# Summing 40 of 72 modulation slots over their row tiles on VectorE in a two-layer diffusion trunk

## The reference, cut to what matters

```python
def adaln(cond, w, b):
    return (jax.nn.silu(cond) @ w + b)[:, None, :]
...
def pre_norm(x, mod, j, g):
    return rmsnorm(x, g) * (1 + mod_chunk(mod, 3 * j + 1)) + mod_chunk(mod, 3 * j)

def post_residual(x, out, mod, j, g, w):
    return x + w * mod_chunk(mod, 3 * j + 2) * rmsnorm(out, g)

def swiglu(h, w_in, w_out):
    gate, up = jnp.split(h @ w_in, 2, axis=-1)
    return (jax.nn.silu(gate) * up) @ w_out
```

## Time and profile before

| | before |
|---|---|
| median of 3 runs | 1670.7 us (1670.51 to 1671.05) |
| span of the profiled execution | 1671.3 us |
| TensorE busy | 1619.9 us, 97% |
| VectorE busy | 834.8 us, 50% |
| ScalarE busy | 695.4 us, 42% |
| DMA | 259.83 MB, mean 155 GB/s |

### The profile page before, as it was taken

How to read it: one execution, slowest core, us unless ns; L and a number is a source line. 1 busy time by engine, 2 the same in 40 slices (tenths; PEclk the granted TensorE clock), 3 DMA queues, 4 the chain that set the end, 5 groups by cost and what they waited for, 6 DMA issues and landing times.

```text
span 1671.3 us, 27671 instructions
## 1 busy us (share of the span) xinstructions
PE 1619.9 (97%) x11325; PEld 1577.4 (94%) x11325; DVE 834.8 (50%) x1323; ACT 695.4 (42%) x1205; POOL 41.9 (3%) x46
## 2 busy tenths in 40 slices
PE   5999999999998999999999999999999999999997
PEld 4999999999887988999999999999999999999997
DVE  5544434463456988443434744433462866343333
ACT  3433333353453456333333633334363356333332
POOL 2000000001100000000000000000000000000000
PEclk8999999999998999999999999999999999999998
DMA  9733366667983126433333633346453465333310
GB/s 326 232 126 125 126 214 221 209 202 220 282 277 101 51 89 192 140 128 127 116 128 126 202 126 125 125 135 193 136 193 126 146 203 181 126 125 119 114 45 38
DMA packets 255663, 259.83 MB, mean 155 GB/s; under 512 B 6625, under 2 KB 253826, under 8 KB 255570
## 3 DMA queue, kind: packets, MB, share of 16 engines
q1 hardware_dynamic: 249664, 251.67, 46.6%
q10 hardware_dynamic: 4978, 4.41, 0.8%
q0 software_dynamic: 928, 2.44, 0.6%
HBM read 255.88 MB, written 2.62 MB: 155 GB/s over the span
## 4 chain that ended last, share of the span: by engine, by line
PE 88%; DVE 7%; issue 2%; ACT 2%; POOL 1%; DMA 1%; ACTq 0%; DVEq 0%; POOLq 0%
PE bank L405 25%; PE bank L406 25%; PE bank L407 25%; PE bank L1454 3%; PE bank L1498 1%; PE bank L426 1%; PE bank L427 1%; PE bank L428 1%; DVE X L1054 1%; DVE WL L372 1%; PE bank L1724 1%; PE bank L1505 1%; DVE HL L1020 1%; ACT WH L358 1%; DVE SUMS L1310 1%
## 5 line engine op out<-in xcount | busy, mean ns | idle before, releaser
L372 DVE TENSOR_TENSOR WL<-RAW,WH 128x1024 fp32r<-128x1024 f32 (+1 forms) x335 | 401.2, 1199 | 693.4 <-ACT WH L358 692.9
L358 ACT ACTIVATE WH<-RAW 128x1024 fp32r<-128x1024 f32 (+1 forms) x344 | 358.2, 1045 | 651.3 <-PE bank L407 638.6
L405 PE MATMUL bank<-HH,WH 128*128 128x384 f32 x1664 | 562.3, 338 | 7.3 <-DVE WL L372 3.1
L406 PE MATMUL bank<-HL,WH 128*128 128x384 f32 x1664 | 559.9, 336 | 0.0
L407 PE MATMUL bank<-HH,WL 128*128 128x384 f32 x1664 | 559.8, 336 | 0.0
L405 PEld LDWEIGHTS bank<-HH,WH 128*128 128x128 f32 x1664 | 313.4, 188 | 10.3 <-DVE WL L372 3.7
L407 PEld LDWEIGHTS bank<-HH,WL 128*128 128x128 f32 x1664 | 313.4, 188 | 0.0
L406 PEld LDWEIGHTS bank<-HL,WH 128*128 128x128 f32 x1664 | 313.3, 188 | 0.0
L405 PE MATMUL bank<-AH,WH 128*128 128x384 f32 x704 | 237.3, 337 | 0.0
L406 PE MATMUL bank<-AL,WH 128*128 128x384 f32 x704 | 236.6, 336 | 0.0
L407 PE MATMUL bank<-AH,WL 128*128 128x384 f32 x704 | 236.6, 336 | 0.0
(11 more groups left out here) (225 smaller groups left out, 1419.3 us busy)
## 6 DMA issues: line engine op xcount, KB each, us to landing
RAW<-in_ffn_w_in SPq DMA_DIRECT2D x88, 1024.0 KB, 5.1
RAW<-in_mod_w SPq DMA_DIRECT2D x72, 1024.0 KB, 6.7
RAW<-in_ffn_w_out SPq DMA_DIRECT2D x32, 1024.0 KB, 5.2
RAW<-in_ab_w_in SPq DMA_DIRECT2D x16, 1024.0 KB, 8.5
RAW<-in_ffn_w_out SPq DMA_DIRECT2D x16, 768.0 KB, 4.7
RAW<-in_cv_w_in SPq DMA_DIRECT2D x12, 1024.0 KB, 6.6
RAW<-in_ab_w_out SPq DMA_DIRECT2D x4, 1024.0 KB, 8.8
RAW<-in_cv_w_out SPq DMA_DIRECT2D x4, 1024.0 KB, 5.4
```

Of the source, the lines that this page charges most:

```text
L358: e.activation(WH[:, (2 * m + b) % 4, 0:nk, :], RAW[:, p, 0:nk, b * P:(b + 1) * P], ACT.Copy).then_inc(half_hi, 1)
L372: e.tensor_tensor(WL[:, k, 0:nk, :], RAW[:, p, 0:nk, b * P:(b + 1) * P], WH[:, k, 0:nk, :].bitcast(F32), ALU.subtract).then_inc(half_ready, 1)
L405: e.matmul(out, WH[:, k, kk, :], xh(kk), start=(first and kk == 0), stop=False)
L406: e.matmul(out, WH[:, k, kk, :], xl(kk), start=False, stop=False)
```

## The change

40 of the 72 slots are no longer multiplied on TensorE. VectorE forms, for each of the two conditions, the sum over the eight row tiles of slot times condition value (a multiplication and seven multiply-adds of 128 x 256 elements per condition: 16 instructions per slot, `mod_sums`). What is left is a 128 x 256 array per condition that has still to be added over its 128 partitions: TensorE does it with four matmuls whose stationary operand is a 128 x 128 block of that array and whose moving operand is one column of ones (`mod_reduce`). The result is already in columns, so the copy of rows and the turn fall away. The other 32 slots stay as they were.

The groups move: s = 0 now carries four groups (`modA`, 16 slots), s = 2 three (`modF`) and s = 3 three (`modG`), ten slots of each in the in-part, one per pair, the rest in the out-part. The attention mixer keeps one group of its six, the convolution none of its own. Coefficients are computed earlier accordingly. The loops over pairs of the in-part are written out, on SyncE too.

```diff
-MOD_GROUPS = {"mod0": 2, "modA": 1, "modK": 1, "modL": 1, "modB": 1, "modC": 6, "modD": 1, "modE": 1, "modG": 1,
-              "modH": 1, "modI": 1, "modJ": 1}
+MOD_GROUPS = {"mod0": 2, "modA": 4, "modB": 1, "modC": 1, "modD": 1, "modF": 3, "modE": 1, "modG": 3, "modH": 1,
+              "modJ": 1}
+SUMMED = {0: "modA", 2: "modF", 3: "modG"}
+SUMMED_OUT = (0, 1, 3, 4, 6, 7)
+SUMMED_IN = 10
...
+            for q in range(SUMMED_IN):
+                order += run(f"in{s}", 2 * q + 4, 2 * q + 6) if q < 9 else run(f"out{s}", 0, 2)
+                order += run(SUMMED[s], q, q + 1)
...
+                    elif kind == "sum":
+                        sp.wait_ge(mod_step, 16 * count)
...
+            def mod_sums(s, q, steps):
+                st, n0 = SUMMED[s], summed_before(s) + q
+                p, uses = ring_at(st, q)
+                a = partial(s, q)
+                if steps[0] == 0:
+                    dve.wait_ge(raw_landed[p], 16 * (uses + 1))
+                    if n0 >= 2:
+                        dve.wait_ge(mod_reduced, n0 - 1)
+                for kk in steps:
+                    for g in range(2):
+                        w, by = RAW[:, p, kk, :], COND[:, kk, g:g + 1]
+                        if kk == 0:
+                            x = dve.tensor_scalar(a[:, g, :], w, by, None, ALU.mult)
+                        else:
+                            dve.wait_ge(mod_step, 16 * n0 + 2 * kk + g - 1)
+                            x = dve.scalar_tensor_tensor(a[:, g, :], w, by, a[:, g, :], ALU.mult, ALU.add)
+                        x.then_inc(mod_step, 1)
...
+                    q = j // 2 - 1
                     nxt[0][0]()
                     nxt[0][1]()
+                    mods(0, 1)
                     for b in range(2):
                         nxt[1][b]()
+                        mods(2 + 2 * b, 3 + 2 * b)
                         dve.wait_ge(silu_done, i * 6 + (2 + base + b + 1))
...
+                    mods(6, 7)
...
+            def mod_reduce(s, q):
+                n0, k = summed_before(s) + q, q // 2
...
+                a = partial(s, q)
+                pe.wait_ge(mod_step, 16 * n0 + 16)
+                for t in range(2):
+                    for g in range(2):
+                        at = 4 * (q % 2) + 2 * t + g
+                        mm = pe.matmul(sum_bank(k)[:, at:at + 1], a[:, g, t * P:(t + 1) * P], ONES[:, 0:1],
+                                       start=True, stop=True)
+                mm.then_inc(mod_reduced, 1)
...
                     for b in range(2):
                         pe.wait_ge(silu_done, i * 6 + (base + b + 1))
                         pe_half(pe, st, 2 * j + b, hh, hl, 8, cols3(bank[b]), True, True, i)
+                        if b == 0 and j >= 4 and s in SUMMED:
+                            mod_reduce(s, j // 2 - 2)
...
-                    elif 3 <= step < 22:
-                        if step == 3:
-                            pe.wait_ge(proj_out, 12)
-                        mod_pair("modC", 4 + 2 * ((step - 3) // 2))
-                    if step % 4 == 0 and step >= 8:
-                        mod_turn(g0 + 1 + (step - 8) // 4)
...
-                pe.wait_ge(conv_step, 4 * 4 + 1)
-                mod_group("modI")
```

More of the change, by code:

```diff
@@ L110, in run @@
         return [(st, n) for n in range(a, b)]
[L112 to L117, removed]
+    order = run("mod0", 0, 2) + run("in0", 0, 2) + run("mod0", 2, 8)
+    for s in range(6):
+        kind = SUBLAYERS[s][0]
+        if s:
+            order += run(f"in{s}", 0, 2) + run(BETWEEN[s - 1], 0, 4)
         if kind == "even":
             order += run(f"in{s}", 2, 6) + run("modC", 0, 2) + run(f"in{s}", 6, 7) + run("modC", 2, 4)
[L120 to L123, removed]
-        else:
-            order += run(f"in{s}", 2, IN_SLOTS[kind])
-        order += run(middle[s][0], 0, middle[s][1]) if s in middle else []
-        order += run(f"out{s}", 0, OUT_SLOTS[kind])
+            order += run(f"in{s}", 7, 16) + run(f"out{s}", 0, 4)
+        elif s in SUMMED:
+            order += run(f"in{s}", 2, 4)
+            for q in range(SUMMED_IN):
+                order += run(f"in{s}", 2 * q + 4, 2 * q + 6) if q < 9 else run(f"out{s}", 0, 2)
+                order += run(SUMMED[s], q, q + 1)
+            for n in range(10):
+                order += run(f"out{s}", n + 2, n + 3)
+                q = SUMMED_IN + SUMMED_OUT.index(n) if n in SUMMED_OUT else None
+                order += run(SUMMED[s], q, q + 1) if q is not None and q < summed_slots(s) else []
+        else:
+            order += run(f"in{s}", 2, IN_SLOTS[kind]) + run(f"out{s}", 0, OUT_SLOTS[kind])
     return order
 def plan():
-    stages, freed, place, split, mod = {}, [], {}, 0, 0
+    stages, freed, place, split, mod, summed = {}, [], {}, 0, 0, 0
     for st, n in ring_order():
@@ L137, in plan @@
         place[st, n] = len(freed)
-        if st.startswith("mod"):
+        if st in SUMMED.values():
+            summed += 1
+            freed.append(("sum", summed))
+        elif st.startswith("mod"):
             mod += 1
@@ L393, in ffn_pairs @@
             after_first()
[L394 to L397, removed]
+            for j in range(2, 22, 2):
+                body(0, j)
         def pe_half(e, st, jj, xh, xl, nk, out, first, last, i=0):
@@ L490, in _ @@
             for st, n in ring_order():
[L491 to L503, removed]
+                wait_ring(place[st, n])
+                load(st, n, *src_of(st, n))
         @block.gpsimd
@@ L1227, in even @@
                         coefficients(g0)
-                    if step % 4 == 3 and step >= 11:
-                        coefficients(g0 + 1 + (step - 11) // 4)
                 assert ticks[0] == 18, ticks
@@ L1581, in ffn @@
                 st = f"out{s}"
-                mods_at = {0: {-1: "modA", 3: "modK", 7: "modL"}, 3: {-1: "modG"}}.get(s, {})
                 def quarter_pair(i, jj):
```

117 lines of the change are left out of this document (72 added, 45 removed).

## The result

| | before | after |
|---|---|---|
| median (range) | 1670.8 us (1670.5 to 1671.1) | 1844.3 us (1843.0 to 1844.8) |
| span of the profiled execution | 1671.3 us | 1841.7 us |

The account below looks back on a forecast made before the run. The prediction took TensorE's instruction stream to bound the kernel. From 1671.3 us it took 37 for removed work and added 36 for one-column matmuls, 97 for stalls and 42 for the clock: 1809 us, range 1765 to 1845.

Parts of the forecast that it names:

- the wait: In-parts of s = 0, 2, 3: TensorE waits 3.6 us (3.2 to 4.6) for the last sum step, 27 times, 97 us.
- Two of the signs: In-parts of s = 0, 2, 3: pairs 21 to 23 us apart; one-column matmuls at 0.107 us an instruction.
- the rival without overlap: VectorE's sum steps take 0.49 to 0.52 us each, stall 4.3 to 4.6, 1828 to 1836 us; chance 0.11, shared with clock losing more.
- I take one such stretch per stall: Behind each of 27 in-part stalls, one half-clock stretch of 3.46 us costs 1.55 us, 42 us in all.
- two stretches per stall: Upper bound of the clock loss behind the 27 in-part stalls: 84 us.
- the rival in which the clock holds: In-part stalls come but the clock does not fall: 1767 us; chance 0.14, including a clock that falls rarely.
- 20.7 - 4 = 16.7: Attention mixer: ten pairs and five turns removed give 20.7 us, less 4 us lost as cover for the softmax chain.
- the first part is wholly on the path: Outside the attention, removing five groups (three in s = 0, one each in s = 3, s = 4) gains 20.5 us in full.
- The likeliest case: In-parts: stall near 3.6 us, clock falling behind nearly all; chance 0.70, own range 1785 to 1830 us.
- the case of 0.11: In-parts: sum steps without overlap or a clock that loses more, 1825 to 1860 us; chance 0.11.
- What was counted at nothing: No cost for transfers of moved slots, written-out loops, ScalarE's changed copies, or the other 13 waits for sums.
- the rival without a stall: In-parts: VectorE has done all 16 steps when TensorE arrives; 1670 us, or 1666 with the mixer's whole gain; chance 0.05.

Follow-up runs that it names:

- the fourth experiment: Changed kernel with the one-column matmuls behind a pair's second half, as in the first experiment, and each issued twice: 1713.0 us, ratio 1.0241 to the kernel before.
- the first experiment: Changed kernel with the four one-column matmuls of an in-part slot moved from behind the next pair's first half to behind its second: 1676.6 us, ratio 1.0025.
- sixth experiments: Changed kernel with sum steps spread on VectorE, none behind the second AL, matmuls at their old place: 1680.3 us, ratio 1.0054 to the kernel before.
- the second experiment: Changed kernel, matmuls at their old place, only four of 16 sum steps behind the fourth split, all behind the second AL: 1760.0 us, ratio 1.0532.
- e2_four_end: The second experiment: changed kernel with four sum steps left behind the fourth split, all behind the second AL; 1760.0 us, ratio 1.0532.
- the fifth experiment: Changed kernel with the step order of e2_four_end; TensorE waits at the old place but issues the one-column matmuls behind the second half: 1724.2 us, ratio 1.0314.
- e3: Changed kernel, matmuls at their old place, only two of 16 sum steps behind the fourth split, both behind the second AL: 1704.3 us, ratio 1.0186.
- e5: The fifth experiment: changed kernel, step order of e2_four_end, wait at the old place, one-column matmuls behind the second half; 1724.2 us, ratio 1.0314.
- e6: As the first experiment, with the sums over partitions packed four side by side and one turn for two slots: 1668.3 us, ratio 0.9974.
- e7: Changed kernel with sum steps spread, none behind the second AL, matmuls at their old place: 1680.3 us, ratio 1.0054.
- e1: The first experiment: changed kernel with the one-column matmuls behind the second half of the next pair; 1676.6 us, ratio 1.0025.
- e4: The fourth experiment: as the first experiment, with each one-column matmul issued twice; 1713.0 us, ratio 1.0241.

## Why the prediction was right, and where it was off

**The mechanism was right.** TensorE's own work does not shrink (the fourth experiment shows it at 0.91 us a slot against 0.93 removed), and the steps queued around the gate and the second AL hold TensorE 27 times (the first and sixth experiments show it: with either end of the wait moved, nearly all of the loss goes). That the number came inside the range is in part luck, as two errors of opposite sign met: the wait was priced 11 us too high and the clock 40 us too low. Released by line 1044, nine times in each of three in-parts, none in the out-parts: as said. Two of the signs came out otherwise, both because of the clock: pairs are 23.5 to 24.1 us apart, but for two, and not 21 to 23, and the one-column matmuls behind a wait take 0.216 us each and not 0.107 (in the first experiment, at the full clock, 0.10).

**The wait: 3.20 us and not 3.6.** Two of its three parts were right: four steps in front of the gate 1.59 us (794.19 to 795.78, forecast 1.6) and the last step's duration of 0.479 (0.48 by the slope from the earlier trace rows). The second AL starts 1.14 us behind the gate where 1.38 was read off: ScalarE's rounding starts 0.58 us behind the gate and the AL 0.56 behind that, where it was 0.69 each in the earlier trace rows. The last step starts at 798.58 and ends at 799.06, and TensorE begins 0.05 us behind it, not 0.2. Together 0.4 us less, 27 x 3.2 = 86 us instead of 97. The bound of 3.2 just held it.

**The steps overlap.** They last 0.479 us and start 0.396 apart, though each signals. So the rival without overlap is out. By the sentence that the prediction took from the Trainium skill, VectorE: DVE Perf Modes, the section on the DRAIN you can't avoid, there would have been 0.48 us or more between starts; this trace does not agree with that sentence alone. The same section adds that an operation which is not held starts earlier, which the prediction left out and with which the 0.396 us agree.

**The clock: the term that was mis-sized.** "I take one such stretch per stall: 27 x 1.55 = 42 us" is the step that failed. The first experiment gives 3.03 us per stall, 82 us in all, nearly the upper bound of two stretches per stall (84): the stretch is 7 us and not 3.46. That it costs 1.55 us when one stretch of 3.46 us follows was right: 1.59 in the second experiment. The 3.46 us were read off, behind a gap of 1.16 us. The 2.46 us of the earlier trace rows stand elsewhere, and they are the idle time of a window, from two gaps; the longer one goes on to 512.41 and lasts 2.35 us. Behind that one the trace of the kernel before has a stretch of more than 6 us at half the clock, which neither the rows nor the prediction took up:

```profile
514.00:520.00 6.00, 5.24 (x20) 3.91 (x19) 2.66 (x5) 3.45 (x7) 0.92 (x1) 0.50 0.64 208
```

Also missing was what stands behind the gap: with 1.5 us of gap the clock fell behind 20 of 27 where one-column matmuls followed (e2_four_end), and behind none where dense ones did (the fifth experiment). Behind 3 us it can fall without one-column matmuls: the changed kernel and the seven made from it each wait 2.99 us in front of the out-projection of s = 4, with dense matmuls of 384 columns behind. The clock fell there in the changed kernel (for 7 us) and in e2, e3, e5, e6 and e7 (for some 3.4 us), and held in e1 and e4. From e1_late and from e5_wait_only:

```profile
1332.39 0.41 PE L446 MATMUL bank<-HH,WH 128*128 128x384 f32 x1 [2.99 <-issue]
```

```profile
1379.79 0.66 PE L446 MATMUL bank<-HH,WH 128*128 128x384 f32 x1 [2.99 <-issue]
```

So what brought the clock down in the 27 stalls can have been the gap alone. Whether the one-column matmuls are why it then stayed down for 7 us, and not for 3.4, is not shown: no run has 27 such gaps with dense matmuls behind. The Trainium skill's TensorE: Matmul & The Clock Gate, under why this matters for your kernels, warns of idle gaps between bursts of matmuls; the trace agrees, with 0.51 behind the wait in the windows above, and the rival in which the clock holds (1767 us) is out.

**The gain.** The mixer got 16.8 us shorter, and 20.7 - 4 = 16.7 were forecast. In s = 4 a step failed: "the first part is wholly on the path, as dense matmuls stand on both sides". The group of slots there should have given 4.1 us and gave none (+1.1). Timelines of TensorE before the out-projection, first of before, then of after, and a window behind it:

```profile
1325.19 0.34 PE L407 MATMUL bank<-HH,WL 128*128 128x384 f32 x1
1325.46 3.70 PE L1454 MATMUL bank<-RAW,COND 128*32 128x128 f32 x128
1329.09 0.44 PE L417 MATMUL bank<-HH,WH 128*128 128x384 f32 x1
```

```profile
1496.16 0.34 PE L436 MATMUL bank<-HH,WL 128*128 128x384 f32 x1
1499.49 0.66 PE L446 MATMUL bank<-HH,WH 128*128 128x384 f32 x1 [2.99 <-issue]
1499.95 0.52 PE L447 MATMUL bank<-HH,WL 128*128 128x384 f32 x1
```

```profile
1499.00:1505.50 6.50, 6.01 (x19) 6.04 (x20) 6.29 (x20) 2.25 (x9) 0.00 (x0) 0.50 0.48 161
```

The four slots filled a wait. Without them VectorE is only then at the convolution's last steps and the splits of the out-projection, and TensorE idles 2.99 us. The clock stands at 0.50 in the window behind that; in the first experiment it held there, and s = 4 came out 2.1 us shorter than here, but still gave only 1.0 of the 4.1. The dense matmuls on both sides showed that TensorE was busy, not that what comes next was ready.

**The sum with the measured terms:** 1671.3 - 37 + 36 + 86 + 82 = 1838, and 5 us more for s = 4 make 1843, beside a span of 1841.7. The median of 1844.3 lies 0.7 us inside the range. With two stretches per stall and the wait as forecast the sum would have been 1851, outside it; the shorter wait made up for that. The likeliest case's own range (1785 to 1830) did not hold the time. It falls into the case of 0.11, in its half with a clock that loses more.

**What was counted at nothing.** Transfers: no engine waits for a slot that it did not wait for before, with 141 GB/s on average over the span. The written-out loops cost some 2 us. TensorE shows no wait for the other 13 slots. In the first experiment, where no wait for the sums is left, this closes the account within some 2 us: forecast were 1 us less than before; s = 4 gives 3.1 us less than its 4.1 (-1.0), the loops cost some 2, and 4.2 us more than before were measured; the mixer, which gave 18.5 us there and not 16.7, is left out of this. It is also why that kernel lies above the 1666 to 1670 us given for the rival without a stall.

## What to carry to other kernels

Before moving work to an engine with spare time, look at what is queued behind it there: 6.4 us of steps in a body in which VectorE was half idle cost 6.2 us per body (the clock's share included), because eight of the sixteen stood between TensorE's own release and the result that it waited for; the same steps ahead of that chain, or the consumer one half later, cost nearly nothing. Price a wait on a saturated TensorE at its length and again at what the clock takes after it, here as much as the wait itself. And count what the moved work leaves behind: a matmul of one column still costs two instructions of 0.106 us here, so TensorE did no less.

## What the runs showed that was not expected

- The clock fell behind 20 of 27 equal gaps (1.45 to 1.54 us with 0.9 us of one-column matmuls behind) and behind none of 27 gaps of the same length with dense matmuls behind. Doubled one-column matmuls without a gap left it at full.
- Behind the gaps of 3.0 to 3.1 us, with one-column matmuls behind them, it stayed low for about 7 us in 25 of 27 cases, twice as long as behind those of 1.5 us (but for one of the 20).
- Behind one gap of 2.99 us with dense matmuls behind it, the same in eight kernels, the clock fell in six and held in two.
- An fp32 matmul of one column costs two instructions of 0.106 us; changing between dense and packed forms costs 0.1 us on either side, as much as two of the packed instructions.
